# An expert MLP's bias: from four small matmuls ahead of a block to two pairs behind its products, and a scatter without dropped rows

## The chip, the cores and the metric

The kernel runs on one core of a Trainium2 chip. The metric is the device time of one execution in microseconds (us); lower is better. PE is TensorE, DVE is VectorE, ACT is ScalarE, POOL is GpSimd, SP is SyncE.

## The reference, cut to what matters

One layer of a hybrid decoder: a mixer (state-space model and short convolution), and then a mixture of experts over 536 tokens (16 + 512 of a prompt, 8 of running sequences), 4 of 32 experts for each token. All data is float32.

```python
def expert_block(args):                 # 128 tokens of one expert
    xe, e = args
    gu = xe @ w_gate_up[e] + b_gate_up[e]       # 1024 -> 2048
    gate, up = gu[:, :D_FF], gu[:, D_FF:]
    gate = jnp.minimum(gate, SWIGLU_LIMIT)
    up = jnp.clip(up, -SWIGLU_LIMIT, SWIGLU_LIMIT)
    h = gate * jax.nn.sigmoid(SWIGLU_ALPHA * gate) * (up + 1.0)
    return h @ w_down[e] + b_down[e]            # 1024 -> 1024
```

The result of each expert is scaled by the token's gate and summed onto the token. The bias that this case is about is `b_gate_up`, 2048 numbers for each of 32 experts.

## The kernel before

There are three stages: the mixer, the router (`router`), and the loop over the experts (`experts`). The router computes the layer's x, the tokens that the experts read (`ffn_in` in DRAM), each token's four experts, and starts the sums in DRAM (`token_sums`) as x. The loop works on one block of up to 128 token slots at a time: block q = 0 to 31 is expert q, block 32 takes tokens beyond 128 of a crowded expert, and more blocks follow only if they are needed.

A block has 24 units (`UNITS`). Units 0 to 7 are the first 512 columns of gate and of up, units 8 to 15 the second 512, units 16 to 23 the product with `w_down`. A unit is 128 rows of weights by 1024 columns. ACT rounds them to a high part (line 1636), DVE subtracts to get the low part (line 1802), in a ring of six slots (`SLOTS`), and PE multiplies in float32r: x high by w high, x high by w low, x low by w high, each into two banks, so six matmuls of 512 columns (line 1737). Gate and up of a half are in banks 2*half and 2*half + 1. Other PE work of a block stands between the units: `select` at unit 8 (line 1715, five small bf16 matmuls that find the next block's token numbers), transposes of h at units 12 and 18 (line 1728), transposes of the next block's x at unit 20 (line 1722).

Each engine's work is written out by hand in its order, with semaphores. When PE has finished 8 units of a half, ACT computes the gate (`gated`, line 1647) and DVE clips up and multiplies (`swiglu`, lines 1820 and 1823).

The bias of an expert is split into three bf16 parts that add up to the float32 value. The router's POOL program computes them and stores them in DRAM (`bias_rows`), and SP loads those of one expert in each block, ahead of the block's weights (`bias_load`, line 948): four groups of 3 rows by 512, at partitions 0, 32, 64 and 96 of a tile. PE waits for this load at the start of the block, and `set_bias` opens the four banks with four matmuls of 3 rows, by a column of ones (line 1744). The products then add to them.

Weights are loaded by SP in eight loads a block (line 944), 12 MB in all: four of 2 MB for gate and up, four of 1 MB for `w_down`; each waits until DVE has finished the units that lay in its place before. The loads for block q + 1 start while PE is at about unit 10 of block q.

POOL gathers the next block's tokens with an indirect DMA (line 1597) and adds the block's result to `token_sums` with another (`scatter`, line 1604). A slot without a token has a row number of 536 or more; both DMAs drop such rows by their bound. At the end SP loads `token_sums`, and a last norm is computed and stored.

Of the kernel before, what the change touches and what calls it, by code (L numbers as in the profile page):

```python
# [14 lines left out]
F32 = mybir.dt.float32  # L15
# [8 lines left out]
P = 128  # L24
D = 1024
# [48 lines left out]
def hybrid_step(nc, a, out):  # L74
    scratch = {
        "u": nc.dram_tensor("u_shuffle", [W, CH, YC], F32).ap(),
        "hf": nc.dram_tensor("ffn_in", [TOK, D], F32).ap(),
        "acc": nc.dram_tensor("token_sums", [TOK, D], F32).ap(),
        "bias": nc.dram_tensor("bias_rows", [E, 4, 3, 512], BF16).ap(),
    }  # L80
    with ExitStack() as ctx:
        def sb(stack, name, shape, dt=F32):
            return stack.enter_context(nc.sbuf_tensor(name, shape, dt))

        def sem(name):
            return ctx.enter_context(nc.semaphore(name))

        bank = [ctx.enter_context(nc.psum_tensor(f"bank{i}", [P, 512], F32)) for i in range(8)]
        keep = {
            "x": sb(ctx, "x", [P, NT, D]),  # L90
            "ident": sb(ctx, "ident", [P, P]),
            "ones": sb(ctx, "ones_col", [P, 1]),
            "conv_ss": sb(ctx, "conv_ss", [P, NT]),
            "pcol": sb(ctx, "pcol", [P, PC]),
                "ring_lo": sb(ctx, "ring_lo", [P, 16, 1024]),
        }
        with ExitStack() as st:
            mid = {
                "ymix": sb(st, "ymix", [P, MT, TOK]),
                "cmix": sb(st, "cmix", [P, MT, TOK]),  # L100
                "w_out": sb(st, "w_out", [P, KD, D]),
            }
            with ExitStack() as s1:
                mixer(nc, a, out, scratch, s1, sb, sem, bank, keep, mid)
            with ExitStack() as s2:

                tables = loop_tables(s2, sb)
                with ExitStack() as s3:
                    router(nc, a, scratch, s3, sb, sem, bank, keep, mid, tables)
                landed = keep["landed"]  # L110

                experts(nc, a, out, scratch, s2, sb, sem, bank, keep, mid, tables, landed)

def mixer(nc, a, out, scratch, stack, sb, sem, bank, keep, mid):

    def buf(name, shape, dt=F32):
# [85 lines left out]
    keep["x_again"] = sem("x_again")  # L202
    keep["x_in"] = x_in
    keep["spent"] = {"g_in": (wglu_in, 16), "sq": (s["gel_sig"], MT), "var": (s["gel_in"], MT), "root": (s["glu_psum"], MT),
                     "fin": (s["y_gelu"], MT), "stored": (s["out_done"], 7 * 16), "step": (s["crow"], 1), "sums": (s["crow_psum"], 1),
                     "bias_in": (s["u_blk_in"], 16 * (CH + 1))}

    def taken(eng, n):

# [705 lines left out]
def loop_tables(stack, sb):  # L915

    return {
        "rank": sb(stack, "rank", [P, NT, E]),
        "slotval": sb(stack, "slotval", [P, NT, E, 2, 3], BF16),
        "iota_s": sb(stack, "iota_s", [P, P]),  # L920
        "one_b": sb(stack, "one_b", [P, 1], BF16),
        "bias": sb(stack, "bias", [P, 512], BF16),
        "over_i": sb(stack, "over_i", [P, 2, NOVER + 1], I32),
        "over_base": sb(stack, "over_base", [P, NOVER + 1]),
        "spare": sb(stack, "spare", [P, 1]),
        "zero": sb(stack, "zero", [P, 1]),
        "idx_next": sb(stack, "idx_next", [P, 1], I32),
        "x_hi": sb(stack, "x_hi", [P, KD, P], F32R),
        "x_lo": sb(stack, "x_lo", [P, KD, P], F32R),
        "w_hi0": sb(stack, "w_hi0", [P, 1, 1024], F32R),  # L930
        "w_lo0": sb(stack, "w_lo0", [P, 1, 1024], F32R),
    }


def weight_load(eng, a, keep, mid, e, j):
# [6 lines left out]
        src = a["w_down"][0].rearrange("e (k p) n -> e p k n", p=P)[e, :, k:k + 2, :]  # L942
        dst = mid["w_out"][:, k:k + 2, :]
    return eng.dma_start(dst, src)


def bias_load(eng, scratch, tb, e, c):
    return eng.dma_start(tb["bias"][32 * c:32 * c + 3, :], scratch["bias"][e, c])


def loop_views(mid):
# [6 lines left out]
def router(nc, a, scratch, stack, sb, sem, bank, keep, mid, tb):  # L958
# [54 lines left out]
    TILES = [NT - 1] + list(range(NT - 1))  # L1013
    Q = NT - 1
    keep["bd_sb"] = sem("bd_sb")
    bias_in, bias_in0 = keep["spent"]["bias_in"]
    keep["bd_added"] = sem("bd_added")
    keep["tiles"] = TILES
    BD_BANK = [1, 2, 3, 4, 5, 0, 1, 2, 4, 5]
# [14 lines left out]
    @block.sync  # L1034
    def _(sp):
        sp.dma_start(w_r[:], a["w_router"][0].rearrange("(k p) e -> p k e", p=P)).then_inc(s["wr_in"], 16)
        sp.dma_start(b_r[:], a["b_router"].to_broadcast([P, E])).then_inc(s["wr_in"], 16)
        sp.dma_start(gffn[:], a["norm_ffn"].to_broadcast([P, D])).then_inc(s["gffn_in"], 16)
        for c in range(P // E):
            sp.dma_start(bdn[c * E:(c + 1) * E, :], a["b_down"][0]).then_inc(s["bdn_in"], 16)  # L1040

        for j in range(4):
            weight_load(sp, a, keep, mid, 0, j).then_inc(keep["landed"][j], 16)
        for q, i in enumerate(TILES):
            sp.wait_ge(s["x_new"], 2 * q + 2)
            sp.dma_start(scratch["acc"][i * P:i * P + rows(i), :], x[0:rows(i), i, :]).then_inc(s["acc_set"], 16)
            sp.wait_ge(s["hf"], q + 1)
            sp.dma_start(scratch["hf"][i * P:i * P + rows(i), :], hf[0:rows(i), q % 2, :]).then_inc(hf_stored[q % 2], 16)
        sp.wait_ge(s["bias_set"], 16 * 4)
        for c in range(4):  # L1050
            bias_load(sp, scratch, tb, 0, c).then_inc(bias_in, 16)
        for c in range(2):
            sp.wait_ge(hf_stored[c], 16 * len(range(c, NT, 2)))
        sp.wait_ge(s["acc_set"], 16 * NT)

    @block.gpsimd
    def _(pool):
# [9 lines left out]
            pool.dma_start(bq[c * E:(c + 1) * E, :], a["b_gate_up"][0][:, c * 512:(c + 1) * 512]).then_inc(s["bias_in"], 16)  # L1067
        g.iota(iota_i[:], pattern=[[1, P]], base=0, channel_multiplier=0)
        g.iota(tok_i[:], pattern=[[P, NT]], base=0, channel_multiplier=1).then_inc(s["tabs"], 1)
        done(g.memset(tb["one_b"][:], 1.0))  # L1070

        pool.wait_ge(s["bias_in"], 64)
        done(g.tensor_scalar(bq[2 * E:4 * E, :], bq[2 * E:4 * E, :], 1.0, None, ALU.add))
        for q in range(3):
            done(g.tensor_copy(bparts[:, q], bq[:]))
            if q < 2:
                done(g.tensor_tensor(bq[:], bq[:], bparts[:, q], ALU.subtract))
        for c in range(4):
            pool.dma_start(scratch["bias"][:, c], bparts[c * E:(c + 1) * E]).then_inc(s["bias_set"], 16)
        pool.wait_ge(s["bias_set"], 16 * 4)  # L1080

        pool.wait_ge(s["mm"], 4 * NT)
        g.memset(xg, 0.0).then_inc(s["xg_clear"], 1)
# [8 lines left out]
    def _(act):  # L1092
# [60 lines left out]
        take_xT(Q)  # L1153
        act.wait_ge(s["gT_psum"], 1)
        nc.scalar.activation(gT[:, 0:Q * P], bank[0][:], ACT.Copy).then_inc(s["gT"], 1)
        act.wait_ge(s["acc_set"], 16 * NT)
        act.wait_ge(s["hf"], NT)
        for j in range(4):
            take_bias(j)
# [316 lines left out]
def experts(nc, a, out, scratch, stack, sb, sem, bank, keep, mid, tb, landed):  # L1476
# [33 lines left out]
    def total(q):  # L1510
# [1 line left out]
        return yo if i == 0 else keep["x"][0:rows(i), i, :]  # L1512

    s = {n: sem("e_" + n) for n in (
        "w_used sel_psum sel bias_used clip sig h hT_psum h_hi h_lo "
        "y_sb y_stored y_out y_free curd turns".split())}
    s.update(keep["loop"])
    block = stack.enter_context(nc.Block())
# [34 lines left out]
    @block.sync  # L1553
    def _(sp):
        def load(e, q):
            sp.wait_ge(s["bias_used"], q)
            for c in range(4):
                bias_load(sp, scratch, tb, e, c).then_inc(t["bias_in"], 16)
            for j in range(LOADS):
                sp.wait_ge(s["w_lo"], UNITS * q + (8 + 2 * j + 2 - UNITS))  # L1560
                weight_load(sp, a, keep, mid, e, j).then_inc(landed[j], 16)
# [28 lines left out]
    def _(pool):  # L1590
# [9 lines left out]
        def scatter(q):  # L1600
# [1 line left out]
            pool.wait_ge(s["y_sb"], q + 1)  # L1602
            pool.sem_inc(s["turns"], 1)
            nc.gpsimd.indirect_dma_start(scratch["acc"], bass.IndirectOffsetOnAxis(ap=row_cur[:, 0:1].bitcast(U32), axis=0), yo, None,  # L1604
                                         bounds_check=TOK - 1, oob_is_err=False, compute_op=ALU.add).then_inc(s["y_stored"], 16)
            pool.wait_ge(s["y_stored"], 16 * q + 16)
            pool.sem_inc(s["y_out"], 1)

# [20 lines left out]
    def _(act):  # L1629
# [11 lines left out]
                nc.scalar.activation(x_hi[:, 4 * h:4 * h + 4, :].rearrange("p k t -> p (k t)"), bank[h][:], ACT.Copy).then_inc(s["x_hi"], 1)  # L1641

        def gated(q, half):
            act.wait_ge(s["w_used"], UNITS * q + 8 * (half + 1))
            if half == 1:
                act.wait_ge(s["h"], 2 * q + 1)
            nc.scalar.activation(g_sb, bank[2 * half][:], ACT.Gelu_apprx_sigmoid).then_inc(s["sig"], 1)  # L1647
# [62 lines left out]
    def _(pe):  # L1710
# [20 lines left out]
        def products(q, j):  # L1731
# [2 lines left out]
            pe.wait_ge(s["w_lo"], UNITS * q + (j + 1))  # L1734
            for first, (v, part) in ((True, (v_hi, high)), (False, (v_hi, low)), (False, (v_lo, high))):
                for u in range(2):
                    last = nc.tensor.matmul(bank[b + u][:], v[:, k, :], part(j)[:, u, :], start=(j == 16 and first),  # L1737
                                            stop=(j in (7, 15, UNITS - 1) and part is high and not first))
            last.then_inc(s["w_used"], 1)

        def set_bias(q):
            pe.wait_ge(t["bias_in"], 64 * q + (t0["bias_in"] + 64))
            for c, b in enumerate((0, 2, 1, 3)):
                last = nc.tensor.matmul(bank[b][:], tb["one_b"][32 * c:32 * c + 3, 0:1].to_broadcast([3, P]),  # L1744
                                        tb["bias"][32 * c:32 * c + 3, :], start=True, stop=False)
            last.then_inc(s["bias_used"], 1)

        def body(q, e_next):
            pe.wait_ge(s["x_lo"], q + 1)
            set_bias(q)  # L1750
            for j in range(UNITS):
                if j == 8:
                    select(e_next, q + 1)
# [8 lines left out]
                if j == 20:  # L1762
                    x_transposes(q + 1)
                    pe.wait_ge(s["h_lo"], 2 * q + 2)
                products(q, j)

        def over(b):
            body(b + E, over_expert(pe, b + 1))

        select(0, 0)  # L1770
        with pe.Fori(0, E - 1) as e:
            body(e, e + 1)
        body(E - 1, over_expert(pe, 0))
        body(E, over_expert(pe, 1))
        overflow(pe, over)

    @block.vector
    def _(dve):
# [37 lines left out]
                            h_hi[:, c, :].rearrange("p k t -> p (k t)").bitcast(F32), ALU.subtract).then_inc(s["h_lo"], 1)  # L1816

        def swiglu(q, half):
            dve.wait_ge(s["w_used"], UNITS * q + 8 * (half + 1))
            v.tensor_scalar(u_sb, bank[2 * half + 1][:], LIMIT + 1.0, 1.0 - LIMIT, ALU.min, ALU.max).then_inc(s["clip"], 1)  # L1820
            dve.wait_ge(s["clip"], 2 * q + half + 1)
            dve.wait_ge(s["sig"], 2 * q + half + 1)
# [98 lines left out]
```

## Time and profile before

| | |
|---|---|
| median of 3 runs | 1492.64 us (1489.88 to 1496.02) |
| profiled execution, its own time | 1492.64 us |
| its span in the profile | 1490.4 us |
| mean granted clock of TensorE | 0.981 of full speed |
| mixer and router | 0 to about 291 us |
| expert loop, 33 blocks | about 291 to 1463 us |
| last sums and norm | 1463 to 1490 us |
| read from and written to device memory | 457.56 MB, 27.82 MB |

The profile records one execution. The span is from its first instruction to its last; the time of an execution is a little longer. An engine's busy time is what its instructions cover; a matmul's recorded end lies well after the next one's start, since matmuls are pipelined, so a rate is read from distances between starts.

### The profile page before, as it was taken

The numbers are of one execution on the slowest core, as the hardware profiler recorded it, in microseconds if no ns is written. First come the engines' busy times: TensorE is split into PE (matmuls) and PEld (weight loads), VectorE is DVE, ScalarE is ACT, GpSimd is POOL, SyncE is SP. The second block draws the span as 40 slices with busy tenths as digits, with TensorE's granted clock in tenths as the row PEclk, the third lists the DMA queues.
The fourth block names the chain that finished last, engine by engine and source line by source line (L and its number), as shares of the span: only waits on it lengthen the run. The fifth ranks groups of instructions, "written<-read, shape, count | busy, mean of one in ns | idle before, by whom it ended". The sixth has DMA issues, their size and how long they took to land.

```text
span 1490.4 us, 22644 instructions
## 1 busy us (share of the span) xinstructions
PE 1431.9 (96%) x7033; PEld 1140.8 (77%) x7034; DVE 1328.2 (89%) x1750; ACT 1030.0 (69%) x1235; POOL 154.9 (10%) x151
## 2 busy tenths in 40 slices
PE   6999899799999999999999999999999999999992
PEld 5888745487888888888888888888888888888882
DVE  5887565699999999999999999999999999999994
ACT  3010332577888888887788888888888888788783
POOL 8100020101000001000000000001100000100000
PEclk9999999699999999999999999999999999999997
DMA  9510482299999999999999999999999999999953
GB/s 304 67 33 1 162 315 93 80 367 411 390 377 363 375 377 368 369 378 378 371 375 374 372 373 377 369 371 372 367 358 362 377 381 372 371 374 373 372 212 120
DMA packets 85285, 469.42 MB, mean 315 GB/s; under 512 B 17934, under 2 KB 19206, under 8 KB 68360
## 3 DMA queue, kind: packets, MB, share of 16 engines
q1 hardware_dynamic: 73160, 447.86, 75.0%
q0 software_dynamic: 12096, 21.18, 6.6%
q8 instruction: 17, 0.28, 0.1%
q14 instruction: 12, 0.10, 0.0%
HBM read 457.56 MB, written 27.82 MB: 326 GB/s over the span
## 4 chain that ended last, share of the span: by engine, by line
PE 75%; DMA 2%; DVE 2%; issue 1%; ACT 0%; SPq 0%; DVEq 0%; ACTq 0%; POOLq 0%
PE bank L1737 70%; PE bank L1722 2%; PE bank L1728 2%; DMA ring_lo<-in_w_gate_up 2%; PE bank L1744 1%; DVE w_lo L1802 1%; DVE x L1883 0%; DMA token_sums<-ymix,row_cur 0%; ACT w_hi L1636 0%; PE bank L1715 0%; DMA ymix<-token_sums 0%; DVE cmix L1823 0%; DVE cmix L1820 0%; DVE ymix L1883 0%; ACT ymix L1674 0%
## 5 line engine op out<-in xcount | busy, mean ns | idle before, releaser
L1802 DVE TENSOR_TENSOR w_lo<-ring_lo,w_hi 128x1024 fp32r<-128x1024 f32 x527 | 618.0, 1221 | 20.1 <-ACT w_hi L1636 10.8
L1636 ACT ACTIVATE w_hi<-ring_lo 128x1024 fp32r<-128x1024 f32 x527 | 544.8, 1059 | 87.7 <-PE bank L1737 64.9
L1737 PE MATMUL bank<-w_hi,x_hi 128*128 128x512 f32 x1056 | 336.7, 400 | 1.1 <-DVE w_lo L1802 1.1
L1737 PE MATMUL bank<-w_lo,x_hi 128*128 128x512 f32 x1056 | 327.4, 391 | 0.0
L1737 PE MATMUL bank<-w_hi,x_lo 128*128 128x512 f32 x1056 | 326.5, 390 | 0.0
L1802 DVE TENSOR_TENSOR w_lo<-w_out,w_hi 128x1024 fp32r<-128x1024 f32 x264 | 311.2, 1221 | 11.4 <-ACT w_hi L1636 11.4
L1636 ACT ACTIVATE w_hi<-w_out 128x1024 fp32r<-128x1024 f32 x264 | 268.0, 1054 | 18.2 <-PE bank L1737 18.2
L1737 PEld LDWEIGHTS bank<-w_hi,x_lo 128*128 128x128 f32 x1056 | 198.8, 188 | 42.9
L1737 PEld LDWEIGHTS bank<-w_lo,x_hi 128*128 128x128 f32 x1056 | 198.8, 188 | 42.8
L1737 PEld LDWEIGHTS bank<-w_hi,x_hi 128*128 128x128 f32 x1056 | 191.4, 189 | 43.3 <-issue 7.7
L1737 PE MATMUL bank<-w_hi,h_hi 128*128 128x512 f32 x528 | 169.0, 401 | 0.0
L1737 PE MATMUL bank<-w_lo,h_hi 128*128 128x512 f32 x528 | 163.6, 391 | 0.0
L1737 PE MATMUL bank<-w_hi,h_lo 128*128 128x512 f32 x528 | 163.1, 390 | 0.0
L1604 POOL DMA_INDIRECT token_sums<-ymix,row_cur x33 | 65.2, 1975 | 725.7 <-ACT ymix L1674 725.7
L1737 PEld LDWEIGHTS bank<-w_hi,h_lo 128*128 128x128 f32 x528 | 99.1, 188 | 21.7
L1737 PEld LDWEIGHTS bank<-w_lo,h_hi 128*128 128x128 f32 x528 | 99.1, 188 | 21.5
L1737 PEld LDWEIGHTS bank<-w_hi,h_hi 128*128 128x128 f32 x528 | 94.3, 189 | 15.9
L1647 ACT ACTIVATE cmix<-bank 128x512 f32<-128x512 f32 x66 | 39.5, 599 | 64.1 <-PE bank L1737 64.1
L506 PE MATMUL bank<-hT,ring_lo 128*128 128x272 f32 x240 | 74.6, 392 | 0.0
L1597 POOL DMA_INDIRECT ymix<-ffn_in,idx_next x33 | 38.9, 1180 | 341.2 <-DVE idx_next L1791 341.2
L505 PE MATMUL bank<-hT,ring_lo 128*128 128x264 f32 x240 | 73.4, 387 | 0.0
L1651 ACT ACTIVATE h_hi<-bank 128x512 fp32r<-128x512 f32 x66 | 39.5, 599 | 47.4 <-PE bank L1728 47.4
(363 smaller groups left out, 1194.3 us busy)
## 6 DMA issues: line engine op xcount, KB each, us to landing
ring_lo<-in_w_gate_up SPq DMA_DIRECT2D x132, 2048.0 KB, 10.9
w_out<-in_w_down SPq DMA_DIRECT2D x132, 1024.0 KB, 13.2
ring_lo<-in_w_in SPq DMA_DIRECT2D x4, 2048.0 KB, 21.8
w_out<-in_w_out SPq DMA_DIRECT2D x2, 2048.0 KB, 8.6
x<-in_x_prompt SPq DMA_DIRECT2D x6, 512.0 KB, 9.0
bias<-bias_rows SPq DMA_DIRECT2D x132, 3.0 KB
token_sums<-x SPq DMA_DIRECT2D x4, 512.0 KB
ffn_in<-hf SPq DMA_DIRECT2D x4, 512.0 KB, 4.6
```

What stands on the lines that cost most here:

```text
L505: nc.tensor.matmul(lo[:, 0:HALF], w_k(k), hT[:, k, 0:HALF], start=(k == 0), stop=(k == KD - 1))
L506: last = nc.tensor.matmul(hi[:, 0:REST], w_k(k), hT[:, k, HALF:TOK], start=(k == 0), stop=(k == KD - 1))
L1597: nc.gpsimd.indirect_dma_start(xg, None, scratch["hf"], bass.IndirectOffsetOnAxis(ap=idx_next[:, 0:1].bitcast(U32), axis=0), bounds_check= ...
L1604: nc.gpsimd.indirect_dma_start(scratch["acc"], bass.IndirectOffsetOnAxis(ap=row_cur[:, 0:1].bitcast(U32), axis=0), yo, None, bounds_check= ...
L1636: nc.scalar.activation(high(j), raw(j), ACT.Copy).then_inc(s["w_hi"], 1)
L1647: nc.scalar.activation(g_sb, bank[2 * half][:], ACT.Gelu_apprx_sigmoid).then_inc(s["sig"], 1)
L1651: nc.scalar.activation(h_hi[:, 4 * half:4 * half + 4, :].rearrange("p k t -> p (k t)"), bank[6 + half][:], ACT.Copy).then_inc(s["h_hi"], 1)
L1722: last = nc.tensor.transpose(bank[k // 4][:, (k % 4) * P:(k % 4 + 1) * P], xg[:, k * P:(k + 1) * P], ident[:])
L1728: last = nc.tensor.transpose(bank[6 + half][:, k * P:(k + 1) * P], h_sb[:, k * P:(k + 1) * P], ident[:])
L1737: last = nc.tensor.matmul(bank[b + u][:], v[:, k, :], part(j)[:, u, :], start=(j == 16 and first), stop=(j in (7, 15, UNITS - 1) and part ...
L1744: last = nc.tensor.matmul(bank[b][:], tb["one_b"][32 * c:32 * c + 3, 0:1].to_broadcast([3, P]), tb["bias"][32 * c:32 * c + 3, :], start=Tr ...
L1802: v.tensor_tensor(low(j), raw(j), high(j).bitcast(F32), ALU.subtract).then_inc(s["w_lo"], 1)
```

## The change

The bias parts of all 32 experts stay on the chip, in a tile of 96 rows (three parts by 32 experts) and 2048 columns, and are no longer loaded from DRAM in each block. A matmul of 96 rows with a column of a table (`pick_row`: ones at rows e, 32 + e and 64 + e) picks and adds up the three rows of expert e. There are four such matmuls a block, two behind unit 7 and two behind unit 15 (`add_bias`), and the products of a half now open their banks themselves. ACT and DVE start on a half when its bias pair is done (`gu_psum`) instead of when its eighth unit is.

In the router, POOL fills the table, and writes the parts with twelve DMAs from one tile to the other instead of four to DRAM.

Apart from the bias, `token_sums` gets 128 more rows, which one more store fills. The scatter's bound now takes them in, so that slots without a token add into them and are not dropped (what they add is the block's result by a gate of zero). The gather still drops them.

```diff
-        "acc": nc.dram_tensor("token_sums", [TOK, D], F32).ap(),
-        "bias": nc.dram_tensor("bias_rows", [E, 4, 3, 512], BF16).ap(),
+        "acc": nc.dram_tensor("token_sums", [TOK + P, D], F32).ap(),
...
-        "one_b": sb(stack, "one_b", [P, 1], BF16),
-        "bias": sb(stack, "bias", [P, 512], BF16),
+        "pick_row": sb(stack, "pick_row", [96, E], BF16),
+        "bias": sb(stack, "bias", [96, 2 * FF], BF16),
...
-def bias_load(eng, scratch, tb, e, c):
-    return eng.dma_start(tb["bias"][32 * c:32 * c + 3, :], scratch["bias"][e, c])
...
             sp.dma_start(scratch["acc"][i * P:i * P + rows(i), :], x[0:rows(i), i, :]).then_inc(s["acc_set"], 16)
+            if i == 0:
+                sp.dma_start(scratch["acc"][TOK:TOK + P, :], x[:, 0, :]).then_inc(s["acc_set"], 16)
...
-        sp.wait_ge(s["bias_set"], 16 * 4)
-        for c in range(4):
-            bias_load(sp, scratch, tb, 0, c).then_inc(bias_in, 16)
         for c in range(2):
             sp.wait_ge(hf_stored[c], 16 * len(range(c, NT, 2)))
-        sp.wait_ge(s["acc_set"], 16 * NT)
+        sp.wait_ge(s["acc_set"], 16 * (NT + 1))
...
-        done(g.memset(tb["one_b"][:], 1.0))
+        done(g.memset(tb["pick_row"][:], 0.0))
+        for q in range(3):
+            v = tb["pick_row"][q * 32:(q + 1) * 32]
+            done(g.affine_select(out=v, in_=v, compare_op=ALU.not_equal, fill=1.0, base=0,
+                                 pattern=[[-1, E]], channel_multiplier=1))
...
-        for c in range(4):
-            pool.dma_start(scratch["bias"][:, c], bparts[c * E:(c + 1) * E]).then_inc(s["bias_set"], 16)
-        pool.wait_ge(s["bias_set"], 16 * 4)
+        for q in range(3):
+            for c in range(4):
+                pool.dma_start(tb["bias"][q * E:(q + 1) * E, c * 512:(c + 1) * 512], bparts[c * E:(c + 1) * E, q]).then_inc(s["bias_set"], 16)
+        pool.wait_ge(s["bias_set"], 16 * 12)
...
-        act.wait_ge(s["acc_set"], 16 * NT)
+        act.wait_ge(s["acc_set"], 16 * (NT + 1))
...
         def load(e, q):
-            sp.wait_ge(s["bias_used"], q)
-            for c in range(4):
-                bias_load(sp, scratch, tb, e, c).then_inc(t["bias_in"], 16)
             for j in range(LOADS):
                 sp.wait_ge(s["w_lo"], UNITS * q + (8 + 2 * j + 2 - UNITS))
                 weight_load(sp, a, keep, mid, e, j).then_inc(landed[j], 16)
...
             nc.gpsimd.indirect_dma_start(scratch["acc"], bass.IndirectOffsetOnAxis(ap=row_cur[:, 0:1].bitcast(U32), axis=0), yo, None,
-                                         bounds_check=TOK - 1, oob_is_err=False, compute_op=ALU.add).then_inc(s["y_stored"], 16)
+                                         bounds_check=TOK + P - 1, oob_is_err=True, compute_op=ALU.add).then_inc(s["y_stored"], 16)
...
         def gated(q, half):
-            act.wait_ge(s["w_used"], UNITS * q + 8 * (half + 1))
+            act.wait_ge(s["gu_psum"], 2 * q + half + 1)
...
@@ -1734,20 +1728,18 @@
             pe.wait_ge(s["w_lo"], UNITS * q + (j + 1))
             for first, (v, part) in ((True, (v_hi, high)), (False, (v_hi, low)), (False, (v_lo, high))):
                 for u in range(2):
-                    last = nc.tensor.matmul(bank[b + u][:], v[:, k, :], part(j)[:, u, :], start=(j == 16 and first),
-                                            stop=(j in (7, 15, UNITS - 1) and part is high and not first))
+                    last = nc.tensor.matmul(bank[b + u][:], v[:, k, :], part(j)[:, u, :], start=(k == 0 and first),
+                                            stop=(j == UNITS - 1 and part is high and not first))
             last.then_inc(s["w_used"], 1)
 
-        def set_bias(q):
-            pe.wait_ge(t["bias_in"], 64 * q + (t0["bias_in"] + 64))
-            for c, b in enumerate((0, 2, 1, 3)):
-                last = nc.tensor.matmul(bank[b][:], tb["one_b"][32 * c:32 * c + 3, 0:1].to_broadcast([3, P]),
-                                        tb["bias"][32 * c:32 * c + 3, :], start=True, stop=False)
-            last.then_inc(s["bias_used"], 1)
-
-        def body(q, e_next):
+        def add_bias(e, b, cols, done):
+            for u in range(2):
+                last = nc.tensor.matmul(bank[b + u][:], tb["pick_row"][:, bass.ds(e, 1)].to_broadcast([96, P]),
+                                        tb["bias"][:, cols[u]:cols[u] + 512], start=False, stop=True)
+            last.then_inc(done, 1)
+
+        def body(q, e, e_next):
             pe.wait_ge(s["x_lo"], q + 1)
-            set_bias(q)
             for j in range(UNITS):
                 if j == 8:
                     select(e_next, q + 1)
@@ -1763,15 +1755,18 @@
                     x_transposes(q + 1)
                     pe.wait_ge(s["h_lo"], 2 * q + 2)
                 products(q, j)
+                if j in (7, 15):
+                    half = j // 8
+                    add_bias(e, 2 * half, (half * 512, FF + half * 512), s["gu_psum"])
 
         def over(b):
-            body(b + E, over_expert(pe, b + 1))
+            body(b + E, over_expert(pe, b), over_expert(pe, b + 1))
 
         select(0, 0)
         with pe.Fori(0, E - 1) as e:
-            body(e, e + 1)
-        body(E - 1, over_expert(pe, 0))
-        body(E, over_expert(pe, 1))
+            body(e, e, e + 1)
+        body(E - 1, E - 1, over_expert(pe, 0))
+        body(E, over_expert(pe, 0), over_expert(pe, 1))
         overflow(pe, over)
...
         def swiglu(q, half):
-            dve.wait_ge(s["w_used"], UNITS * q + 8 * (half + 1))
+            dve.wait_ge(s["gu_psum"], 2 * q + half + 1)
```

## Rows read from the trace of the kernel before

**Rows 1.** The page: busy time, share of the span and instructions of each engine.

```profile
PE 1431.9 (96%) x7033; PEld 1140.8 (77%) x7034; DVE 1328.2 (89%) x1750; ACT 1030.0 (69%) x1235; POOL 154.9 (10%) x151
```

**Rows 2.** Windows of the expert loop: busy time by engine, granted clock, DMA share.

```profile
core 0: us, PE busy (x) PEld busy (x) DVE busy (x) ACT busy (x) POOL busy (x), PEclk, DMA share, GB/s
368.00:1463.00 1095.00, 1095.00 (x5239) 889.83 (x5235) 1055.45 (x1144) 884.67 (x987) 98.42 (x62) 1.00 0.92 364
1216.00:1251.00 35.00, 35.00 (x169) 28.61 (x165) 33.82 (x38) 28.64 (x32) 3.19 (x2) 1.00 0.98 378
```

**Rows 3.** Chain of waits in one block: start us, length us, what.

```profile
791.91 0.33 PE bank L1744 x4
...
817.69 0.43 PE bank L1728 x4
...
827.25 0.33 PE bank L1744 x4
```

**Rows 4.** Timeline of PE around the bias matmuls: start us, us, instruction.

```profile
791.52 0.39 PE L1737 MATMUL bank<-w_hi,h_lo 128*128 128x512 f32 x1
791.84 0.39 PE L1744 MATMUL bank<-bias,one_b 3*128 3x512 bf16 x4
...
792.16 0.73 PE L1737 MATMUL bank<-w_hi,x_hi 128*128 128x512 f32 x2
792.74 0.63 PE L1737 MATMUL bank<-w_lo,x_hi 128*128 128x512 f32 x2
...
802.75 0.61 PE L1737 MATMUL bank<-w_hi,x_lo 128*128 128x512 f32 x2
```

**Rows 5.** Timeline of PE around the select matmuls.

```profile
802.97 0.39 PE L1737 MATMUL bank<-w_hi,x_lo 128*128 128x512 f32 x1
803.20 0.28 PE L1715 MATMUL bank<-slotval,cmix 128*128 x5
...
803.34 0.71 PE L1737 MATMUL bank<-w_hi,x_hi 128*128 128x512 f32 x2
803.89 0.62 PE L1737 MATMUL bank<-w_lo,x_hi 128*128 128x512 f32 x2
```

**Rows 6.** Line 1744, weight load and matmul: duration ns min/median/max.

```profile
L1744 PEld LDWEIGHTS bank<-bias,one_b x132: 90/91/101, 291.4 to 1427.9; 3*128 3x128 bf16 x132
L1744 PE MATMUL bank<-bias,one_b x132: 384/385/604, 291.4 to 1427.9; 3*128 3x512 bf16 x132
```

**Rows 7.** Waits in the loop: waiter, releaser, total us, times, longest.

```profile
DVE cmix L1820 <- PE bank L1737: 0.4, 2, 0.2
```

**Rows 8.** Timeline of DVE in one block, second gate half.

```profile
815.01 0.69 DVE L1820 TENSOR_SCALAR cmix<-bank 128x512 f32<-128x512 f32 x1
815.73 0.69 DVE L1823 SCALAR_TENSOR_TENSOR cmix<-cmix 128x512 f32<-128x512 f32 x1
```

**Rows 9.** DMA in 12.1 us around the scatters at 1219 and 1465: packets, MB, share.

```profile
q0 software_dynamic: 144, 0.52, 27.5%
token_sums<-ymix,row_cur POOLq DMA_INDIRECT x1, 6.8
...
q0 software_dynamic: 144, 0.08, 4.9%
```

**Rows 10.** Issues from 343 us; the last one's us to landing; ACT's use.

```profile
343.00 9.13 SPq L944 DMA_DIRECT2D ring_lo<-in_w_gate_up  x4
...
ring_lo<-in_w_gate_up SPq DMA_DIRECT2D x1, 2048.0 KB, 17.9
...
370.64 2.01 ACT L1636 ACTIVATE w_hi<-ring_lo 128x1024 fp32r<-128x1024 f32 x2 [0.50 <-ACT ymix L1674]
```

**Rows 11.** Chain of waits at the end.

```profile
1465.47 4.49 DMA token_sums<-ymix,row_cur
```

**Rows 12.** Timeline of POOL in the router stage.

```profile
210.21 2.06 POOL L1079 DMA_DIRECT2D bias_rows<-bparts  x4 [0.29 <-POOL bparts L1075]
268.23 0.95 POOL L1083 MEMSET ymix<- 128x1024 f32 x1 [55.96 <-PE bank L1201]
```

More of the change, by code:

```diff
@@ L204, in mixer @@
     keep["spent"] = {"g_in": (wglu_in, 16), "sq": (s["gel_sig"], MT), "var": (s["gel_in"], MT), "root": (s["glu_psum"], MT),
-                     "fin": (s["y_gelu"], MT), "stored": (s["out_done"], 7 * 16), "step": (s["crow"], 1), "sums": (s["crow_psum"], 1),
-                     "bias_in": (s["u_blk_in"], 16 * (CH + 1))}
+                     "fin": (s["y_gelu"], MT), "stored": (s["out_done"], 7 * 16), "step": (s["crow"], 1), "sums": (s["crow_psum"], 1)}
     def taken(eng, n):
@@ L1015, in router @@
     keep["bd_sb"] = sem("bd_sb")
-    bias_in, bias_in0 = keep["spent"]["bias_in"]
     keep["bd_added"] = sem("bd_added")
@@ L1514, in experts @@
     s = {n: sem("e_" + n) for n in (
-        "w_used sel_psum sel bias_used clip sig h hT_psum h_hi h_lo "
+        "w_used sel_psum sel gu_psum clip sig h hT_psum h_hi h_lo "
         "y_sb y_stored y_out y_free curd turns".split())}
```

## The prediction

> **What bounds the kernel now.** I read the page first, for who is busy: PE 96% of the span, VectorE (DVE) 89%, ScalarE 69% [rows 1]. Then the windows, to see if that holds where the change works: from 368 to 1463 us PE is busy 1095.00 of 1095.00 us at full granted clock (2.4 GHz), DVE 1055 us, ScalarE 885 us, and the DMA engines 0.92 of the time [rows 2]. Then the chain of waits through one block: it is PE from end to end, and one block lies between two bias groups, 827.25 - 791.91 = 35.34 us [rows 3]. So anything that PE has to do more per block is paid once per block, unless it is hidden by a gap, and there is none. Last, the timeline of PE at the two places where its stream changes its kind, since durations of single matmuls overlap and only distances between starts are time [rows 4, 5]. From the start at 792.74 to the one at 802.75 lie 44 product matmuls: 10.01 / 44 = 0.2275 us each [rows 4].
>
> **PE: the bias leaves the start of the block.** The four old matmuls read 3 rows each, from partitions 0, 32, 64 and 96, into four banks. The trace has them as one group of four that starts at 791.84 and is over in 0.39 us, although one alone lasts 0.385 us [rows 4, 6]: they run side by side. Their whole price is the distance over the place: from the last product before (791.52) to the third after (792.74) 1.22 us, of which three product steps are 3 x 0.2275 = 0.68. The old bias costs **0.54 us per block**, about 0.10 of it as a pause before the group (791.52 + 0.23 = 791.75, start at 791.84).
>
> **PE: the bias comes back as two pairs.** Each new matmul reads 96 rows, so two of them can't have rows of their own, as the old four had; I take them to run one after another, like products. No row shows a bf16 matmul of 512 columns alone in the stream. The nearest row is the step of the float32 products, 0.2275 us [rows 4]; at the granted 2.4 GHz these are 546 cycles for 512 columns, about one a column, and just one would make 0.213. I take 0.2275, since no row shows less for so many columns, and 4 x 0.2275 = 0.91. Next, the change of kind. Around the five select matmuls the stream goes to bf16 and back: start to start 803.89 - 802.97 = 0.92, less 0.68, is 0.24 us, with no pause on entering (803.20 - 802.97 = 0.23), 0.14 for the five, and 0.32 instead of 0.23 for the first product after, so 0.09 for coming back [rows 5]. The first pair stands right ahead of select and shares that return; the second pair has its own: 0.09. New price 0.91 + 0.09 = 1.00, change **+0.46 us per block**. Lower bound: four steps of 0.213 with no return, 0.85 - 0.54 = +0.31. Upper bound: each weight load of 0.091 us [rows 6] stands bare ahead of its matmul, 4 x 0.304 + 0.09 = 1.31, so +0.77; a pause of 0.10 on entering each pair would give +0.65 and lies inside.
>
> The Trainium skill, page "TensorEngine Tiling (Array Packing)", section Tiling Modes, says that tiles of 32 rows operate independently and that changing the mode drains the engine. The trace agrees in both: four in the time of one, and a pause of 0.10 us that the select group doesn't have [rows 4, 5]. By that rule the pause goes with the old form and the fourfold overlap goes too; it speaks against the change.
>
> Of 33 blocks, 31 (from the third on) run with PE as the bound. The first two don't: PE stands there for weights, and in them both the old group and the new pairs lie beside other work; in the first the old group leaves ahead of the gate half and 0.46 comes in before it, which cancels within 0.2 us. So 31 x 0.46 = **14.3 us** (9.6 to 23.9).
>
> **Who waits for the pairs.** ScalarE and DVE start on a gate half behind the pair instead of behind the eighth product unit, 0.46 us later. PE is held by the same 0.46, so their distance to PE's next need does not shrink. The tightest such distance: DVE finishes the second half at 815.73 + 0.69 = 816.42 and PE's transposes of it run at 817.69, 1.27 us later [rows 3, 8]. DVE waits for PE at this place only 0.4 us in 62 times [rows 7]; it is busy 34.1 of 35.34 us, and the longer block gives it 0.46 more. Cost: none, as long as that 1.27 stands.
>
> **The scatter writes all 128 rows.** Slots without a token pointed beyond the tensor and were dropped; now they add into 128 spare rows. On average 536 x 4 / 33 = 65 rows were real, so 63 more of 4 KB move per block. The trace has nearly full scatters already: one with 0.52 MB lands in 6.8 us at 27.5% of 16 engines in 12.1 us, one with 0.08 MB takes 4.9% [rows 9]. So a row costs 22.6% x 12.1 x 16 / 107 = 0.41 us of one engine, and 63 of them 26 us, 1.6 us of all sixteen. Blocks now keep the DMA busy 0.92 x 35.34 = 32.5 us; 34.1 of 35.8 afterwards. The block with the 0.52 MB scatter did so already: DMA share 0.98, PE busy 35.00 of 35.00 [rows 2]. Nothing in the loop then. Two places are not covered. Early on, the weight queue is still behind: the last load issued from 343 us leaves at about 352 and lands 17.9 later, at 369.7, and ScalarE takes it at 370.64 [rows 10], 0.9 us of margin against some 2 us of added rows ahead of it. DVE's 1.27 us takes most of that: **0.5 us**, 0 to 3. And the last scatter lies on the path: 4.49 us for 0.08 MB [rows 9, 11]. A full one lands in 6.8 us, among weight loads that are absent at the end, so I take 6.8 - 4.5 = **2.3**. Below, 0 (the loads explain it all); above, 3.3, the whole 27.5% of 12.1 us that the full scatter takes of the engines, on top.
>
> **What costs nothing.** GpSimd issues twelve loads instead of four (2.06 us for four, so 4 us more) and fills a small table, but waits 55.96 us afterwards for PE [rows 12]; without that cover it would be some 6 us. The extra 512 KB store on SP's queue comes before 220 us and nobody waits for its landing until the last store, 50 us later. SP sheds four bias loads and a wait per block; SP isn't on the chain. The bias no longer passes through a load per block, whose landing PE waited for, but PE never stood for it in the loop (busy 1095.00).
>
> **Sum.** 14.3 + 0.5 + 2.3 = 17.1. The profiled execution took 1492.64 us, which is also the median of the three runs: 1492.64 + 17.1 = **1509.7 us**, +1.1%. About 0.5% (7.5 us) is what a measurement of this kernel can tell from no change.
>
> **Rivals.** (a) Cheap pairs: the two matmuls of a pair, to different banks, overlap as the old four did, so a pair costs one step: 2 x 0.2275 + 0.09 = 0.55, change 0; with the scatter's 2.3, 1494.9 us. For it: the old group shows that overlap exists. Against: those had disjoint rows; the products also alternate banks and don't overlap [rows 4]. The Trainium skill, page "TensorE: Matmul & The Clock Gate", section Back-to-back issue gap, gives 0.131 us per matmul of 512 columns in a stream with weight loads; by it the four would cost 0.52 + 0.09 - 0.54 = +0.07 per block, 2 us in all, also no measurable change. The trace's 0.2275 for float32 data does not agree, and no row shows bf16. Chance 0.10.
> (b) DMA becomes the bound: if a row to the spare region costs twice the 0.41 us, the added work is 3.2 us and a block needs 35.7, at the edge; at three times, 37.3 us against 35.8, 31 x 1.5 = 47 us more than the forecast, about 1556; just over the edge, 1525 to 1530. For it: share 0.98 in a full block. Against: that block held. Chance 0.07.
> (c) Faster: the pairs vanish in the products' stream. Place: the two joints on PE; it decides when the four new matmuls together cost under 0.54 - (7.5 + 2.3) / 31 = 0.22 us, 55 ns each. For it: five select matmuls take 0.14 us. Against: those have 6 columns, not 512. At 0.14 for the four: 31 x -0.40 + 0.5 + 2.3 = -9.6, 1483.0 us. Chance 0.03.
>
> **How the numbers follow.** My forecast, pairs in series, has 0.80 and alone reaches from 1492.64 + 9.6 = 1502 to 1492.64 + 23.9 + 3 + 3.3 = 1523. To hold 8 in 10 with a margin I widen to 1498 (half way to rival a) and 1524. Slower by over 0.5% (above 1500.1): 0.80 + 0.07 = 0.87; within: 0.10; faster: 0.03.
>
> **What would show it.** Right: in the changed profile the four bias matmuls start about 0.22 us apart, in two pairs; the distance between the same line in two blocks is 35.8 us; PE stays 100% busy; the scatters show 0.52 MB each, 6.8 us. Wrong: starts of a pair together (rival a), PE waiting for DVE or DVE for ScalarE for the DMA and a DMA share of 1.00 (rival b), or a block below 35.2 us (rival c). If DVE's distance to the transposes of the second half has gone from 1.27 us to nothing, my "no cost" for the later gate was the false step.

## The result, and the profile after

The changed kernel takes 1503.41 us (median of 5 runs, 1502.61 to 1506.3) against 1492.86 us before (5 runs): 1.0076 of the time, 95% interval 1.0058 to 1.0093, so 10.5 us or 0.8% slower. The forecast was 17.1 us slower, in a range of 5 to 31.

The profile of the changed kernel is of an execution of 1507.43 us, span 1505.3 us. Of its 14.9 us over the span before, about 3 arise before the expert loop: the first product starts at 294.94 us instead of 291.98. This is not the price of the new router code: in the profile of e3 below, which has the same router, the first product starts at 291.32. Below, blocks and stretches are compared, not spans.

From the page: busy time by engine, and the queue of the indirect DMAs (packets, MB, share of 16 engines).

```profile
PE 1441.7 (96%) x7033; PEld 1149.0 (76%) x7034; DVE 1321.2 (88%) x1750; ACT 1025.0 (68%) x1235; POOL 161.2 (11%) x162
...
q0 software_dynamic: 12352, 29.68, 10.0%
```

The window over the same stretch of the loop as in [rows 2]: busy time of PE, its weight loads, DVE, ACT and POOL, granted clock, DMA share, GB/s.

```profile
368.00:1463.00 1095.00, 1095.00 (x5190) 891.13 (x5190) 1045.12 (x1139) 876.35 (x982) 98.61 (x62) 1.00 0.97 372
```

PE is still busy all of the time at full clock. The DMA share went from 0.92 to 0.97; the queue of the indirect DMAs carries 29.68 MB instead of 21.18.

The chain of waits through one block, to be held against [rows 3] (start, length, what; line 1737 is the new bias matmul, 1709 select, 1731 the products, 1722 the transposes of h):

```profile
809.84 0.45 PE bank L1737 x2
810.29 0.11 PE bank L1709 x5
810.39 5.56 PE bank L1731 x24
...
821.86 0.45 PE bank L1737 x2
...
825.06 0.44 PE bank L1722 x4
...
845.48 0.45 PE bank L1737 x2
```

From one first pair to the next: 845.48 - 809.84 = **35.64 us**, 0.30 more than 35.34. Over the 31 blocks in which PE is the bound, with the unrounded mean lengths of 35.645 and 35.335 us, this is 31 x 0.31 = 9.6 us (9.3 by the 0.30).

The timeline of PE at the second pair and, below it, at the first pair and select, as in [rows 4, 5]:

```profile
821.47 0.39 PE L1731 MATMUL bank<-w_hi,x_lo 128*128 128x512 f32 x1
...
821.70 0.61 PE L1737 MATMUL bank<-bias,pick_row 96*128 96x512 bf16 x2
821.96 0.82 PE L1731 MATMUL bank<-w_hi,h_hi 128*128 128x512 f32 x2
822.61 0.62 PE L1731 MATMUL bank<-w_lo,h_hi 128*128 128x512 f32 x2
...
809.45 0.39 PE L1731 MATMUL bank<-w_hi,x_lo 128*128 128x512 f32 x1
...
809.68 0.61 PE L1737 MATMUL bank<-bias,pick_row 96*128 96x512 bf16 x2
810.12 0.27 PE L1709 MATMUL bank<-slotval,cmix 128*128 x5
810.25 0.71 PE L1731 MATMUL bank<-w_hi,x_hi 128*128 128x512 f32 x2
810.80 0.62 PE L1731 MATMUL bank<-w_lo,x_hi 128*128 128x512 f32 x2
```

A narrower window shows the second matmul of the second pair by itself:

```profile
821.93 0.38 PE L1737 MATMUL bank<-bias,pick_row 96*128 96x512 bf16 x1
```

So the two matmuls of a pair start at 821.70 and 821.93, 0.23 us apart, and not together. (The record of the next product starts at 821.96 already, but lasts 0.58 us instead of 0.39, so its start says little; a distance over several steps is safer.) From 821.47, the last product of a half, to 822.61 there are five steps (two bias matmuls, three products): 1.14 / 5 = 0.228 us, the plain step of the products. There is no pause ahead, and the products behind are not late.

Each one alone, by the view of its line (ns, minimum, median, maximum), is recorded as long as one of the old four [rows 6]. Recorded ends of matmuls are modelled, so this alone proves little; e6 below compares 96 rows with 3 by starts.

```profile
L1737 PE MATMUL bank<-bias,pick_row x132: 379/384/391, 308.6 to 1463.5; 96*128 96x512 bf16 x132
```

The waits in the loop: DVE now stands 25.2 us for the pair at the gate half, where it stood 0.4 us for the products [rows 7]. PE waits for DVE nowhere.

```profile
DVE cmix L1815 <- PE bank L1737: 25.2, 30, 0.8
```

The distance that the prediction named for the later gate holds: DVE finishes the second half at 823.07 + 0.69 = 823.76 and PE's transposes start at 825.06, 1.30 us later, where it was 1.27.

The last scatter, in the DMA view (packets, MB, share; us to landing) and in the chain at the end:

```profile
q0 software_dynamic: 144, 0.52, 51.4%
token_sums<-ymix,row_cur POOLq DMA_INDIRECT x1, 6.1
```

```profile
1478.31 6.09 DMA token_sums<-ymix,row_cur
```

All 128 rows go out, 0.52 MB, and it takes 6.09 us on the path instead of 4.49 [rows 11].

### The profile page after: what moved, and what is told of

Read it like the earlier page. It is cut to its first block, busy times and chain, and to the rows that moved or that the text cites. A ratio compares the mean times of both kernels' runs of the same rounds, so it can differ in the third digit from the quotient of the medians.

```text
span 1505.3 us, 22244 instructions
## 1 busy us (share of the span) xinstructions
PE 1441.7 (96%) x7033; PEld 1149.0 (76%) x7034; DVE 1321.2 (88%) x1750; ACT 1025.0 (68%) x1235; POOL 161.2 (11%) x162
## 3 DMA queue, kind: packets, MB, share of 16 engines
q0 software_dynamic: 12352, 29.68, 10.0%
## 4 chain that ended last, share of the span: by engine, by line
PE 77%; DVE 1%; issue 1%; DMA 1%; ACT 0%; SPq 0%; ACTq 0%; POOLq 0%; DVEq 0%
PE bank L1731 71%; PE bank L1716 2%; PE bank L1737 2%; PE bank L1722 2%; DMA token_sums<-ymix,row_cur 0%; DVE x L1878 0%; DVE w_lo L1797 0%; DMA ymix<-token_sums 0%; ACT w_hi L1630 0%; PE bank L1709 0%; DVE cmix L1818 0%; DVE cmix L1815 0%; DVE ymix L1878 0%; ACT ymix L1668 0%; DVE ssf L68 0%
## 5 line engine op out<-in xcount | busy, mean ns | idle before, releaser
L1797 DVE TENSOR_TENSOR w_lo<-ring_lo,w_hi 128x1024 fp32r<-128x1024 f32 x527 | 609.5, 1219 | 10.0 <-ACT w_hi L1630 9.9
L1731 PE MATMUL bank<-w_hi,x_hi 128*128 128x512 f32 x1056 | 332.3, 396 | 1.1 <-DVE w_lo L1797 1.0
L1731 PE MATMUL bank<-w_hi,h_hi 128*128 128x512 f32 x528 | 175.4, 413 | 0.0
```

Of the source, the lines that this page charges most:

```text
L1797: v.tensor_tensor(low(j), raw(j), high(j).bitcast(F32), ALU.subtract).then_inc(s["w_lo"], 1)
```

## The experiments

Block lengths are read like the two above: the distance between the same piece in two blocks.

**e1: the bias part of the change alone.** The scatter, its bound and the sums as before.

```diff
-        "acc": nc.dram_tensor("token_sums", [TOK + P, D], F32).ap(),
+        "acc": nc.dram_tensor("token_sums", [TOK, D], F32).ap(),
...
-                sp.dma_start(scratch["acc"][TOK:TOK + P, :], x[:, 0, :]).then_inc(s["acc_set"], 16)
...
-                                         bounds_check=TOK + P - 1, oob_is_err=True, compute_op=ALU.add)
+                                         bounds_check=TOK - 1, oob_is_err=False, compute_op=ALU.add)
```

> The changed kernel with the scatter, its bound and the sums' rows as before. Theory P (PE pays for four bias matmuls in series): block length stays 35.64 us, the last scatter falls back to about 4.5 us on the path, and the time is 9 to 10 us above the kernel before (ratio about 1.006). Rival D (the cost is the scatter's extra rows and a fuller DMA): block falls back to 35.34 us and the time to that of the kernel before (ratio 1.000).

1501.47 us, ratio 1.0056 (1.0044 to 1.0069), 8.6 us more than before. The chain, in the loop and at the end:

```profile
808.59 0.45 PE bank L1735 x2
844.23 0.45 PE bank L1735 x2
...
1477.05 4.45 DMA token_sums<-ymix,row_cur
```

The block stays 35.64 us without the full scatter, and the last scatter is back at 4.45. Rival D of this experiment, that the cost is the scatter's, is out.

**e2: the scatter part alone**, on the kernel before.

```diff
-        "acc": nc.dram_tensor("token_sums", [TOK, D], F32).ap(),
+        "acc": nc.dram_tensor("token_sums", [TOK + P, D], F32).ap(),
...
+                sp.dma_start(scratch["acc"][TOK:TOK + P, :], x[:, 0, :]).then_inc(s["acc_set"], 16)
...
-                                         bounds_check=TOK - 1, oob_is_err=False, compute_op=ALU.add)
+                                         bounds_check=TOK + P - 1, oob_is_err=True, compute_op=ALU.add)
```

> The kernel before with only the new scatter: 128 more rows of sums, one more store, and its bound. Theory P: block 35.34 us, last scatter 6.1 us instead of 4.5, in all 1.6 us more (ratio 1.001). Rival D: block about 35.6 us and 9 to 10 us more (ratio 1.006).

1494.56 us, ratio 1.0007 (0.9998 to 1.0016): 1.7 us, at the edge of what can be told.

```profile
792.74 0.33 PE bank L1746 x4
828.08 0.33 PE bank L1746 x4
...
1466.32 5.97 DMA token_sums<-ymix,row_cur
```

Block 35.34 us, last scatter 5.97. The window over the loop shows the DMA share at 0.97 with the shorter block too, and PE without a gap:

```profile
368.00:1463.00 1095.00, 1095.00 (x5239) 889.47 (x5238) 1056.23 (x1145) 885.33 (x988) 98.05 (x62) 1.00 0.97 372
```

The two parts alone add up to 8.6 + 1.7 = 10.3 us; the whole change cost 10.5.

**e3: the changed kernel without bias matmuls.** The bias of gate and up is left out of the result.

```diff
-                if j in (7, 15):
-                    half = j // 8
-                    add_bias(e, 2 * half, (half * 512, FF + half * 512), s["gu_psum"])
...
-            act.wait_ge(s["gu_psum"], 2 * q + half + 1)
+            act.wait_ge(s["w_used"], UNITS * q + 8 * (half + 1))
```

> The changed kernel without its bias matmuls: the bias of gate and up is left out of the result, and the gate half waits for the eighth unit again. Theory P: the block falls by what the four cost, 4 x about 0.22 = 0.88 us, to 34.76 us, still all PE, which also prices the old group at 35.34 - 34.76 = 0.58; the time is about 31 x 0.58 = 18 us less than before, plus 1.6 of the scatter: 1476.5 us, ratio 0.989. Rival V (DVE is the next bound right below): DVE is busy 34.1 us a block, so if its waits don't shrink the block stops at 35.0 or above and PE shows gaps.

1476.02 us, ratio 0.9888 (0.9872 to 0.9903). The chain at select, in two blocks:

```profile
795.17 0.12 PE bank L1709 x5
829.90 0.12 PE bank L1709 x5
```

829.90 - 795.17 = 34.73 us a block, and PE is still busy 1072.00 of 1072.00 us from 368 to 1440, so rival V (DVE as the next bound) is out at this length. This prices both forms from the same base: the old group 35.34 - 34.73 = **0.61 us**, the two pairs 35.64 - 34.73 = **0.91 us**, four plain steps.

**e4: the pairs ahead of their halves.**

```diff
-                products(q, j)
-                if j in (7, 15):
+                if j in (0, 8):
                     half = j // 8
                     add_bias(e, 2 * half, (half * 512, FF + half * 512), s["gu_psum"])
+                products(q, j)
```

Here the pairs open the banks, and the gate half waits for the eighth unit.

> The changed kernel with each pair ahead of its half instead of behind it: ahead of unit 0 and, next to select, ahead of unit 8; the gate waits for the eighth unit as before. Theory P: the place doesn't matter, block 35.64 us (35.60 to 35.68), and ScalarE's and DVE's waits at the gate half shrink by some 0.45 us each. Rival G (the later start of the gate half costs PE time): block about 35.4 us or less.

One run, 1501.8 us, beside 1492.89 before; with a single run the time is weak, and the block length is the evidence.

```profile
795.33 0.45 PE bank L1737 x2
806.68 0.12 PE bank L1709 x5
806.80 0.45 PE bank L1737 x2
807.25 5.45 PE bank L1731 x24
830.88 0.45 PE bank L1737 x2
```

830.88 - 795.33 = 35.55 us, 0.09 less than the changed kernel and outside the 35.60 to 35.68 that I expected; not the 35.4 of rival G either. The chain shows where. Select now stands ahead of a bias pair, not ahead of a product, and the 24 products that follow take 5.45 us instead of the changed kernel's 5.56: 0.11 less, which is the whole difference, while select and the pairs last as long as before (0.01 apart). In the changed kernel the second product behind select starts 0.32 us after the first, as in [rows 5]; here two bias matmuls of 512 columns lie between select and the product. DVE's wait at the gate half is 12.2 us over the same stretch instead of 25.2, and PE's chain has no gap in either kernel that this could have closed. The place of a pair matters by what it separates, not by what waits for it.

**e5: the old matmuls on separate strips, as pairs** behind unit 7 and unit 15; ACT and DVE wait for the pair, as in the changed kernel. (A strip is one of the four stretches of 32 partitions.)

```diff
-            for c, b in enumerate((0, 2, 1, 3)):
+            for c, b in ((half, 2 * half), (half + 2, 2 * half + 1)):
                 last = nc.tensor.matmul(bank[b][:], tb["one_b"][32 * c:32 * c + 3, 0:1].to_broadcast([3, P]),
-                                        tb["bias"][32 * c:32 * c + 3, :], start=True, stop=False)
+                                        tb["bias"][32 * c:32 * c + 3, :], start=False, stop=True)
...
-            sp.wait_ge(s["bias_used"], q)
+            sp.wait_ge(s["bias_used"], 2 * q)
```

> The kernel before with its own matmuls of 3 rows at partitions 0, 32, 64 and 96, but as two pairs behind unit 7 and unit 15, gate half waiting for them. Theory J (a group of matmuls on separate strips of 32 rows pays a fixed price for the two changes of form, about 0.25 us, and one step of 0.32 whether it holds two or four): each pair costs 0.57, two 1.14, block 34.77 + 1.14 = 35.91 us, so slower than the changed kernel's 35.64; ratio to before about 1.012. Rival S (the price is only one matmul step per group): two pairs cost 0.45 to 0.5, block 35.25 us, a little faster than before.

1721.69 us, ratio 1.1543 (1.1525 to 1.156). Neither theory. The timelines of PE and of SP's queue, one piece of the chain of waits, the waits of SP, and one wait of ACT:

```profile
826.80 0.39 PE L1743 MATMUL bank<-bias,one_b 3*128 3x512 bf16 x2
827.12 0.73 PE L1737 MATMUL bank<-w_hi,h_hi 128*128 128x512 f32 x2
...
827.36 1.58 SPq L948 DMA_DIRECT2D bias<-bias_rows  x4
829.21 2.14 SPq L944 DMA_DIRECT2D ring_lo<-in_w_gate_up  x4
...
831.02 20.09 DMA ring_lo<-in_w_gate_up
...
SPq L948 <- PE bank L1743: 846.8, 29, 30.1
...
ACT w_hi L1636 <- DMA ring_lo<-in_w_gate_up: 280.2, 116, 3.7
```

What the pairs cost by themselves, e8 shows. The loss is elsewhere: there is one tile for the bias, so the next expert's load waits for the second pair, at 827.2, and SP's eight weight loads stand behind that wait in its queue. In the kernel before, the block that starts at 791.91 lets them go from 800.55 on, 8.6 us into the block, when PE has done about six of its units (the "unit 10" of the kernel's description is DVE's). Here they go at 829.21, behind PE's sixteenth unit. The chain then runs through their 20.09 us to landing, and ACT stands 280 us for weights. I had moved a wait on an engine whose queue I didn't read.

**e6: the old four on one strip**, at the old place; the tile is now 3 rows by four groups of 512.

```diff
-    return eng.dma_start(tb["bias"][32 * c:32 * c + 3, :], scratch["bias"][e, c])
+    return eng.dma_start(tb["bias"][:, c, :], scratch["bias"][e, c])
...
-                                        tb["bias"][32 * c:32 * c + 3, :], start=True, stop=False)
+                                        tb["bias"][:, c, :], start=True, stop=False)
```

> The kernel before with the four groups of 3 bias rows all at partitions 0 to 2, so that the four matmuls share one strip of 32 rows; place and number stay. If it is the separate strips that let the old four run together, they now start about 0.22 us apart: 3 more steps, 3 x 0.22 = 0.66, block 35.34 + 0.66 = 36.0 us, time 20 us above before. If few rows alone make a matmul cheap: block stays 35.34.

1512.68 us, ratio 1.0136 (1.012 to 1.0151), 20 us more.

```profile
800.54 0.96 PE bank L1744 x4
836.50 0.96 PE bank L1744 x4
```

Block 35.96 us, the group 0.96 us instead of 0.33 in the chain, with the number, the rows of each and the place in the block unchanged. The separate strips are what let four matmuls run in the time of one. In series, three rows or 96 make no difference to a step: (0.96 - 0.33) / 3 = 0.21 us here, 0.23 in the changed kernel.

The same run parts the overlap from the joints, the places where the stream goes over into the group and back. Four matmuls of 3 rows in series cost 35.96 - 34.73 = 1.23 us, four of 96 rows in series 0.91. The 0.32 between them is at the joints: from the last product to the first bias matmul 836.44 - 836.12 = 0.32 us instead of 0.23, from the last bias matmul to the first product 837.40 - 837.10 = 0.30, and from that to the second product 0.34. So the joints come with the 3-row form, whether its matmuls overlap or not.

**e7: select beside the old group.** The kernel before; DVE makes the rows for select one block earlier (the tables of the overflow blocks get one entry more).

```diff
             set_bias(q)
+            select(e_next, q + 1)
             for j in range(UNITS):
-                if j == 8:
-                    select(e_next, q + 1)
...
-            pick(e_next, base)
...
                     take_slots(q + 1)
+                    pick(e_next, base)
...
-            body(e, e + 1, zero[:, 0:1], True)
+            body(e, e + 2, zero[:, 0:1], True)
```

> The kernel before with the five select matmuls moved from unit 8 to right behind the old bias group at the start of the block (DVE picks their rows a block earlier), so that the stream leaves the product matmuls once less. Theory J: one return of 0.09 to 0.11 us with its slow restart is saved, block about 35.2 to 35.25 us, time 3 to 4 us less than before, ratio 0.998. If each kind of matmul pays its own return wherever it stands: block 35.34, ratio 1.000.

1487.96 us, ratio 0.9974 (0.9964 to 0.9983): 3.8 us faster than the kernel before. This and e9, at the same ratio, are the fastest complete versions here.

```profile
789.43 0.33 PE bank L1744 x4
789.76 0.21 PE bank L1715 x5
...
1422.79 0.33 PE bank L1744 x4
```

(1422.79 - 789.43) / 18 = 35.19 us a block, 0.15 less than before. So kinds of matmul that stand together share a return to the products; that each pays its own is out. Theory J gave 0.09 to 0.11 for it; the other 0.05 stays open.

**e8: e5 with the bias loads moved in SP's queue** behind the sixth weight load, and PE's wait for them at unit 7.

```diff
+                if j == 5:
+                    sp.wait_ge(s["bias_used"], 2 * q)
+                    for c in range(4):
+                        bias_load(sp, scratch, tb, e, c).then_inc(t["bias_in"], 16)
...
+                if j == 7:
+                    pe.wait_ge(t["bias_in"], 64 * q + (t0["bias_in"] + 64))
```

> As e5 (two pairs of 3-row matmuls on separate strips, behind unit 7 and unit 15), but SP issues the next expert's bias loads behind the sixth weight load instead of ahead of the first, so that the weight loads no longer queue behind the wait for the second pair, and PE waits for them only at unit 7. If the wait on SP's queue was the whole of e5's loss, the block is all PE again. Theory J (a strip group costs its two changes of form and one step, whether two or four matmuls): 34.74 + 2 x 0.60 = 35.94, or 0.1 less for the pair that stands next to select, 35.84 us; ratio 1.010 to 1.012. Rival S (a pair costs one step of about 0.25): 35.25 us, ratio 0.998.

1509.1 us, ratio 1.0105 (1.0088 to 1.0123). The chain in the loop, and its longest piece early on:

```profile
813.28 0.32 PE bank L1744 x2
813.60 0.21 PE bank L1716 x5
...
825.27 0.32 PE bank L1744 x2
849.00 0.32 PE bank L1744 x2
...
322.33 24.42 DMA bias<-bias_rows
```

Block 849.00 - 813.28 = 35.72 us, all PE again: what e5 lost beyond its pairs came from the bias loads ahead of the weight loads in SP's queue. (e8 moved PE's wait too, but PE waits for no bias load in the profile of e5.) Two strip pairs cost 35.72 - 34.73 = 0.99 us, a little more than the changed kernel's two pairs in series at 0.91. This is less than theory J's 35.84 us and far from rival S. The block is worth 31 x 0.38 = 12 us of the 16. Early on, the bias load landed after 24.42 us behind six weight loads, and PE stood 1.87 us for it at unit 7; in all, from the first product to the third select, e8 took 90.84 us (294.05 to 384.89) and the kernel before 87.36 (291.98 to 379.34), so 3.5 us lie there.

**e9: e7 with select ahead of the group.**

```diff
-            set_bias(q)
             select(e_next, q + 1)
+            set_bias(q)
             for j in range(UNITS):
```

> As e7, with select ahead of the bias group at the start of the block instead of behind it. If what e7 saved is one exposed return to the products, order doesn't matter: block 35.18 us. If the pause ahead of a strip group is the drain of the last 512-column matmul, it shrinks behind the short select matmuls, and the block is 35.10 us or less. If a short matmul ahead of a product exposes the product's weight load and a strip group does so more, 35.2 to 35.25.

1489.24 us, ratio 0.9974 (0.9964 to 0.9983).

```profile
792.28 0.12 PE bank L1715 x5
792.41 0.33 PE bank L1744 x4
827.49 0.12 PE bank L1715 x5
```

827.49 - 792.28 = 35.21 us. The order inside the place makes 0.02 us, and nothing that the times can tell apart. The expectation of 35.10 or less, a pause that shrinks behind the short matmuls, is out; the other two, 35.18 and 35.2 to 35.25, lie too close together for this run to choose.

## Why the prediction was right, and where its sizes were off

- **PE is the bound, and the pairs are paid once per block.** Right: PE is busy all of the steady loop in every version but e5, and the block moved by what PE got to do.
- **The old group, 0.54 us.** Too small: 0.61 by e3. I took three steps around the group for its whole price. The ten product steps from 792.74 to the start below, in the timeline of before, take 2.30 us, 0.03 more than ten plain ones, and that looks like part of it; where the other 0.04 lies is open.

```profile
795.04 0.62 PE L1737 MATMUL bank<-w_hi,x_hi 128*128 128x512 f32 x2
```

- **The new pairs, 0.91 plus a return of 0.09.** The 0.91 is what e3 measured. The return was the failed term. I had put select's 0.09 down to the change from bf16 to float32. The timeline after shows that 512-column bf16 matmuls go over into the products at no cost, and e4 that the cost behind select goes away when such matmuls stand between. So what costs is a product right behind very short matmuls, or behind 3-row ones (e6). That its weight load lies bare there is my reading of the starts; no run tests it.
- **So +0.46 us per block** was +0.30, 14.3 us in all some 9.5, at my lower bound of 9.6, which assumed steps of 0.213 and an old group of 0.54; neither is so. Both errors, 0.07 and 0.09, point the same way. With 31 x 0.16 = 5 us they are most of the 6.6 us between forecast and result. The mechanism held and its size was at the edge of what I allowed.
- **The later gate costs nothing.** Right. DVE's wait at the gate grew to 25.2 us, PE never waited for DVE in the loop, and the distance ahead of the transposes went from 1.27 to 1.30 us; e4 took half of the wait away and gained only the joint.
- **The full scatter in the loop costs nothing.** Right (e2: block 35.34, DMA share 0.97 where I worked out 0.95). Rival (b) had no part in it.
- **The early weight queue, 0.5 us.** Not seen: from the first product to the third select e2 takes 87.19 us (292.97 to 380.16) and the kernel before 87.36. A load that PE itself waits for is another matter there, as e8's 3.5 us show.
- **The last scatter, 2.3 us.** 1.6 in the changed kernel, 1.5 in e2; at the end, where no weight loads run, it lands in 6.1 us, sooner than the 6.8 that I took.
- **The router's extra work costs nothing.** Right as far as it can be seen: POOL's twelve loads are issued in 5.98 us, and it waits 53.7 us for PE afterwards; e3 has the same router and starts its loop no later than the kernel before.
- **Rivals (a) and (c).** The starts of a pair, 0.23 us apart, and the 0.91 us of the four refute both; e6 shows that the old four's overlap belongs to their strips.

The order of causes is shown by e1, e2 and e3, and e6 shows that the joints come with the 3-row form. Why such a group has a pause of 0.10 ahead of it and a late product behind it is not shown. The Trainium skill, page "TensorEngine Tiling (Array Packing)", section Tiling Modes, says that a change of the tiling mode drains the engine; the pause in [rows 4] and its absence ahead of the 96-row pairs (821.47 to 821.70, a plain step) agree.

## What to carry to other kernels

Small matmuls on separate strips of rows share one step; when they are rewritten as one taller matmul each, the rows are free but the steps are paid, one for each. The gain of the overlap is bought with two joints, so here it paid for a group of four (0.61 us against 0.91) and not for two groups of two (0.99 against 0.91). Put very short matmuls beside other small ones rather than between products (e4, e7), and before a wait is moved, read what is queued behind it.

## What the runs showed of the hardware that I had not expected

- A group on separate strips costs 0.61 us for four matmuls of 512 columns (e3), and about 0.5 a pair (e8), against 0.91 for four in series, though the four overlap fully. About half of the group's price is its joints, 0.32 us by e6.
- The change between bf16 and float32r matmuls costs nothing measurable: five steps across it take 1.14 us, as many as five plain ones.
- The bias load, 12 KB in four pieces, lands after 24.42 us behind six weight loads that left in the 15 us before it (e8).
